# The lo part of every second block of v moves from VectorE to GpSimd, behind a gather

## The reference

```python
expert = jnp.take_along_axis(cand_i, best_pos, axis=-1)
gates = jax.nn.softmax(best_v, axis=-1).astype(h.dtype)
...
ub = jnp.take(u, eb, axis=0)
hid = jax.nn.gelu(jnp.einsum('tkd,td->tk', ub, xb), approximate=False) * gb
vb = jnp.take(v, eb, axis=0)
return jnp.einsum('tk,tkd->td', hid, vb)
```

## Time and profile before

| | us |
|---|---|
| three runs: median (lowest to highest) | 3398.58 (3393.21 to 3403.74) |
| the profiled execution, its own time | 3402.77 |
| its span, first to last instruction | 3401.0 |
| mean granted TensorE clock, share of full speed | 0.973 |
| busy in the span: TensorE matmuls | 3249.2 (96%) |
| VectorE | 2045.5 (60%) |
| ScalarE | 1330.5 (39%) |
| GpSimd | 593.9 (17%) |

### The profile page before, as it was taken

How to read it: one execution, slowest core, us unless ns; L and a number is a source line. 1 busy time by engine, 2 the same in 40 slices (tenths; PEclk the granted TensorE clock), 3 DMA queues, 4 the chain that set the end, 5 groups by cost and what they waited for, 6 DMA issues and landing times.

```text
span 3401.0 us, 40709 instructions
## 1 busy us (share of the span) xinstructions
PE 3249.2 (96%) x16107; PEld 2690.4 (79%) x16107; DVE 2045.5 (60%) x3541; ACT 1330.5 (39%) x2339; POOL 593.9 (17%) x573
## 2 busy tenths in 40 slices
PE   8999999999999999999799998899998999989998
PEld 5764899998888888888688885788787667778887
DVE  5766887876888888888655436445543345443333
ACT  3131238883444444444322225454443124233322
POOL 0001349971222222221000000000000000000000
PEclk9999999999999999999899998999998999989999
DMA  7426244569999999997255422121221122222322
GB/s 258 131 79 230 75 139 160 208 236 343 336 326 334 337 327 331 337 332 278 90 184 185 160 79 89 59 90 63 75 85 58 39 86 76 93 81 94 99 93 80
DMA packets 190206, 574.40 MB, mean 169 GB/s; under 512 B 16576, under 2 KB 82112, under 8 KB 171712
## 3 DMA queue, kind: packets, MB, share of 16 engines
q1 hardware_dynamic: 152144, 367.96, 31.6%
q0 software_dynamic: 37872, 203.84, 16.6%
HBM read 523.89 MB, written 47.84 MB: 168 GB/s over the span
## 4 chain that ended last, share of the span: by engine, by line
PE 82%; DVE 7%; ACT 4%; DMA 3%; POOL 2%; issue 1%; SPq 0%; DVEq 0%; ACTq 0%; POOLq 0%
PE ps L237 11%; PE ps L238 11%; PE ps L239 11%; PE ps L1627 5%; PE ps L1628 5%; PE ps L1626 5%; PE ps L1382 4%; PE ps L1384 4%; PE ps L1383 4%; PE ps L602 2%; PE ps L246 2%; DMA hidden_dram<-peerg_HS 2%; PE ps L171 1%; DMA adaw_AW<-w_ada 1%; PE ps L605 1%; PE ps L2289 1%
## 5 line engine op out<-in xcount | busy, mean ns | idle before, releaser
L229 DVE TENSOR_TENSOR Wl<-W,Wh 128x1024 fp32r<-128x1024 f32 (+2 forms) x337 | 407.6, 1210 | 694.5 <-ACT Wh L217 694.4
L217 ACT ACTIVATE Wh<-W 128x1024 fp32r<-128x1024 f32 x363 | 377.5, 1040 | 553.5 <-PE ps L239 519.2
L1382 PE MATMUL ps<-peer_Hh,Wh 128*128 128x384 f32 x1024 | 348.3, 340 | 2.7 <-DVE Wl L229 1.9
L1384 PE MATMUL ps<-peer_Hh,Wl 128*128 128x384 f32 x1024 | 344.5, 336 | 0.0
L1383 PE MATMUL ps<-peer_Hl,Wh 128*128 128x384 f32 x1024 | 344.0, 336 | 0.0
L1595 POOL DMA_INDIRECT peerv_UV<-peer_uv,peer_EX x128 | 209.3, 1635 | 639.4 <-DVE peer_Y L1663 583.9
L1626 PE MATMUL ps<-peerv_VH,peer_HTh 128*128 128x512 f32 x768 | 299.0, 389 | 2.5 <-DVE peer_HTl L1689 2.5
L1628 PE MATMUL ps<-peerv_VH,peer_HTl 128*128 128x512 f32 x768 | 300.5, 391 | 0.0
L1627 PE MATMUL ps<-peerv_VL,peer_HTh 128*128 128x512 f32 x768 | 300.2, 391 | 0.0
L237 PE MATMUL ps<-f_Hh,Wh 128*128 128x512 f32 x672 | 262.3, 390 | 2.2 <-DVE Wl L229 2.2
L239 PE MATMUL ps<-f_Hh,Wl 128*128 128x512 f32 x672 | 261.5, 389 | 0.0
(11 more groups left out here) (497 smaller groups left out, 6530.2 us busy)
## 6 DMA issues: line engine op xcount, KB each, us to landing
W<-peer_u SPq DMA_DIRECT2D x128, 512.0 KB, 6.9
peerv_VR<-peer_v SPq DMA_DIRECT2D x128, 512.0 KB, 5.3
gates_dram<-peerg_GB SPq DMA_DIRECT2D x12, 2048.0 KB, 7.3
peerv_GR<-gates_dram SPq DMA_DIRECT2D x32, 768.0 KB, 8.3
f_AW<-w_ada POOLq DMA_DIRECT2D x48, 512.0 KB, 4.3
W<-w_gate SPq DMA_DIRECT2D x44, 512.0 KB, 3.2
W<-w_up SPq DMA_DIRECT2D x44, 512.0 KB, 3.3
swa_AW<-w_ada POOLq DMA_DIRECT2D x32, 512.0 KB, 4.3
```

Source lines behind the costliest of these rows:

```text
L217: A.then_inc(e.activation(w_parts(i)[0], w_raw(i), ACT.Copy), ("w_hi", i))
L229: (G if i in lo_on_pool else V).then_inc(e.tensor_tensor(lo, w_raw(i), hi.bitcast(F32), SUB), ("w", i))
L1382: e.matmul(o, hi[:, k, :], H2[0][:, k, 0:TD], start=k == 0, stop=False)
L1384: ins = e.matmul(o, lo[:, k, :], H2[0][:, k, 0:TD], start=False, stop=k == 7)
```

## The change

For odd j, `v_lo(j)` is made by GpSimd. It stands in GpSimd's order right behind the issue of gather j+4 (`v_lo(k - 4)` behind `uv_load(e, k)` for odd k from 5 on), and for j = 125 and 127 behind the last gather. VectorE keeps the even blocks. Who waited for the lo part of v (the load j+3 of v on the sync engine, and `b(j)` on TensorE) waits for GpSimd's semaphore for odd j, through the new helper `v_split`. Each `v_lo(j)` from j = 2 on also waits for `b(j-2)`, whose matmuls read the buffer of `VL` that it writes.

```diff
     def v_load(e, j):
         if j < 128:
             if j >= 3:
-                V.wait_ge(e, ("vl", j - 3))
+                v_split(e, j - 3)
             else:
                 V.wait_ge(e, "EX")
...
+    def v_split(e, j):
+        (G if j % 2 else V).wait_ge(e, ("vl", j))
+
     def v_lo(e, j):
         A.wait_ge(e, ("vh", j))
-        V.then_inc(e.tensor_tensor(VL[:, j % 2, :], VR[:, j % 3, :], VH[:, j % 2, :].bitcast(F32), SUB), ("vl", j))
+        if j >= 2:
+            PE.wait_ge(e, ("b", j - 2))
+        (G if j % 2 else V).then_inc(e.tensor_tensor(VL[:, j % 2, :], VR[:, j % 3, :], VH[:, j % 2, :].bitcast(F32), SUB), ("vl", j))
...
             uv_load(e, k)
+            if k >= 4 and k % 2:
+                v_lo(e, k - 4)
+        for j in (125, 127):
+            v_lo(e, j)
...
                 n = j - 1
                 s = n % 2
-                V.wait_ge(e, ("vl", n))
+                v_split(e, n)
                 V.wait_ge(e, ("htl", n))
...
-            v_lo(e, j)
+            if j % 2 == 0:
+                v_lo(e, j)
             if j:
                 y_add(j - 1)
```

## The result

| | before | after |
|---|---|---|
| median of four runs, us | 3398.19 | 3445.47 |
| lowest to highest | 3393.21 to 3403.74 | 3442.21 to 3448.81 |
| the profiled execution, its own time | 3402.77 | 3442.21 |
| its span | 3401.0 | 3440.4 |
| first matmul of b(0) to first matmul of b(127) | 824.7 | 869.9 |

The changed kernel is slower: 3445.47 against 3398.19, ratio 1.0132 with a 95% interval of 1.012 to 1.0145, so +47 us where 29 were forecast. The stage itself is 45.2 us longer. (The two profiled spans differ by 39.4 only, because behind b(127) this execution of the changed kernel was 6.1 us shorter, 1775.9 against 1781.9, in a part that the change doesn't touch.)

A forecast was written before the change was run, and what follows sets the result against it. TensorE's matmuls were taken to bound the dense stage. New TensorE waits of 22 or 34 us plus 1 at the start gave 23 to 35, middle 29, on a median of 3398.6: 3427.6 us, range 3402 to 3456.

The forecast's parts named there:

- TensorE bounds, no gain possible: In the dense-expert stage TensorE's matmuls set the time without gaps, so moving work off VectorE can gain nothing.
- The relief of 0.7 us: In odd blocks, with the subtraction gone from VectorE, y_add starts sooner and the round is 0.7 us shorter.
- The hold: GpSimd's subtraction shuts out VectorE's instructions that read two SBUF tiles, for 2.11 us each.
- case (a): Subtraction follows the gather with no gap, ahead of htl, and holds VectorE; htl is done 4.77 us after y_add(j-1) ends.
- The round of two blocks: VectorE and ScalarE's ring over two blocks: 11.96 us without gap, plus 1.14 where w_lo is in the even round.
- The round against TensorE: Slower rounds from b(7) to b(19) make TensorE wait 2.4 or 3.7 us in each 14 blocks, 22 or 34 in all.
- The lead before the change: In the kernel before, operands of b(19) were ready at about 67.5 us, 3.0 us early.
- Small items: At the start b(1) waits, +1 us; later loads stay hidden, and the next gather and waits for b(j-2) cost nothing.
- case (b): With a 0.3 us gap behind the gather, GpSimd gets in after htl(j) and holds VectorE from 2.76 to 4.87 us.
- The waits absorb it: Rival: GpSimd's hold falls in VectorE's waits or is partial, so the ring stays ahead; 3399 to 3406 us, chance 0.16.
- GpSimd is shut out too: Rival: GpSimd's subtraction misses the gap behind htl and comes behind tg, 5 us later; 3450 to 3700 us, chance 0.08.
- Faster: Rival: only if TensorE had hidden gaps; 3380 to 3388 us, chance 0.03.

The follow-up runs named there:

- experiment 5: Changed kernel, but GpSimd makes only the 17 blocks with j % 14 = 7 or 13: 3398.48 us, ratio 0.9997 to the kernel before.
- experiment 9: Changed kernel, but in odd blocks GpSimd copies VR into VL instead of subtracting, reading one tile: 3403.28 us, ratio 1.0003 to the kernel before.
- experiment 2: Changed kernel, but in odd blocks GpSimd fills VL by two memsets of zeros and reads nothing: 3404.96 us, ratio 1.0008 to the kernel before.
- experiment 3: Kernel before, plus 62 GpSimd subtractions of one tile from itself into a scratch tile, which no other engine waits for: 3444.33 us, ratio 1.0122.
- 7: Changed kernel, but each of GpSimd's 64 subtractions also waits for tg of its block: 3436.16 us, ratio 1.0108 to the kernel before.
- 8: Changed kernel, but the subtraction stands ahead of the gather's issue in GpSimd's order: 3440.74 us, ratio 1.0118 to the kernel before.
- experiment 4: Changed kernel, but GpSimd makes only the 32 blocks with j % 4 = 1: 3428.3 us, ratio 1.0079 to the kernel before.

## Why the prediction was right, and why it was too low

**TensorE bounds, no gain possible: right.** With the earlier trace rows as they were, no kernel came out faster; the lowest ratios are 0.9997 and 1.0003 (experiments 5 and 9).

**The relief of 0.7 us: right.** It shows in experiment 2 (+0.7 of lead) and in experiment 9, where it pays for a hold of 0.66.

**The hold: right.** Read from one pair of rows of another stage as 2.11 us; it measured 2.03 on an htl. (The prediction set the 2.11 beside an estimate of 2.1 us for the length of a subtraction; 2.11 is the length of the hold, and the subtraction itself takes 2.36 alone and 2.40 here.) The hold was measured alone (experiment 3), without reading (2), with one input (9) and at other steps (7, 8). The Trainium skill, "SBUF — State Buffer", section "Who interferes with whom", says that a VectorE instruction with two SBUF inputs contends with a GpSimd instruction only where that one reads SBUF; the trace agrees at both ends, 0.56 us beside a memset and 1.22 beside a copy.

**Where it falls: right, case (a),** in 51 of 64 blocks: gap 0.02 us, GpSimd's subtraction 2.40 against 2.36, htl ready at 4.80 against 4.77. In two more, 53 and 109, GpSimd came behind the start of htl and held it too. Nine others held tg. The last two, for which the prediction had noted "no gather ahead" and nothing else, held y_add:

```profile
1658.50 3.11 DVE L1672 SCALAR_TENSOR_TENSOR peer_Y<-peerv_UV,peerv_HG,peer_Y 128x1024 f32<-128x1024 f32 x1 [0.81 <-ACT peerv_HG L1655]
```

**The round of two blocks: right,** 13.13 against 13.10.

**The round against TensorE: right in kind, too low in size.** I walked the slower rounds in one line from b(7) to b(19) and had TensorE wait 2.4 us in 14 blocks (operands at 72.9, TensorE at 70.5). Experiment 7, where no tg and no y_add is held, has 3.37. The same stretch one period on, from the end of b(21) to b(33), says where the 0.97 are; there the end of b(21) is at 946.22 (VectorE, then TensorE):

```profile
1017.03 2.60 DVE L1701 TENSOR_TENSOR peer_HTl<-peer_TG,peer_HTh 128x384 fp32r<-128x384 f32 x1 [0.59 <-ACT peer_HTh L1668]
```

```profile
1019.77 0.47 PE L1637 MATMUL ps<-peerv_VH,peer_HTh 128*128 128x512 f32 x1 [0.46 <-DVE peer_HTl L1701]
```

The htl of block 33 is done after 73.4 us and not 72.9: the five rounds take 12.95, 12.93, 13.13, 13.42 and 13.13 us where the forecast had 12.91 twice and 13.10 three times, and the long one is the round in which v_hi(30) waits for b(28), a wait that the walk left out. TensorE would have come after 70.3 us and not 70.5 (kernel before: 936.53 to 1006.84). The handover of 0.14 us was not in the sum, nor the 0.1 us that TensorE loses behind its stops. These add up to 0.94 of the 0.97. That TensorE stands at several blocks and not at one adds nothing to the sum by itself; it makes b(28) later, and with it, probably, the fourth round (no run tells this from the rest).

**The lead before the change: wrong, and not a term of the sum.** The prediction had the operands of b(19) "about 67.5, 3.0 us early". In the trace of before, one period on, the htl is ready at 70.0 and b(33) starts at 70.3. The rounds from v_hi(23) to v_hi(33) take 12.4 us each, and the fourth 13.9, where I had 12.1 and 12.3: v_hi(j) waits for b(j-2), ScalarE stands there for 1.59 us ahead of v_hi(30), and the ring can't run further ahead. I had read these waits (33.5 us in 53 places) as a lead of 0.26 a block; what is left in front of b is 0.27 us in four blocks of 14. The forecast's 2.4 is the slow ring less TensorE's own time and doesn't use the 3.0, so this error did not move it; it is what made the expectation of experiment 4 wrong. Rows that showed it were at hand: the end of htl and the start of b of a few blocks.

**The GELU: not in the prediction.** The tg waits for ScalarE in a block where VectorE, relieved of v_lo, comes sooner than TensorE and ScalarE deliver (experiment 2: 0.71 us sooner). A quarter of a microsecond there lets GpSimd in before tg (tg starts 0.6 and not 0.9 us ahead of the subtraction). 1.3 us in 14 blocks.

**Small items.** b(1) was late by 1.29 us (forecast +1). The loads stayed hidden. GpSimd's next gather didn't wait for its subtraction.

The stage's 45.2 us by these terms: 23 were forecast in case (a) (22 and 1 for the start); the longer wait in each 14 blocks adds 9.7 (experiment 7's stage is 857.4, +32.7); the held tg add 12.5. The forecast's middle of 29 had case (b) in it, which did not occur. The two errors have the same sign, and the range of 3402 to 3456 held 3445 because it also spanned the rivals, not because its bounds knew of them.

**The rivals.** *The waits absorb it* fell: htl is longer in all the odd blocks where it isn't tg or y_add. But its idea, that a hold can fall in a lead, is true for the blocks of experiment 5, and its lateness of VL shows by itself in experiment 2. *GpSimd is shut out too* fell: 64 subtractions have a mean of 2.403 us against 2.36 alone. *Faster* fell.

## What to carry to other kernels

Before moving a step between VectorE and GpSimd, ask of each instruction that runs beside it whether both read SBUF; here GpSimd's subtraction of 2.4 us held a VectorE instruction that came during it until shortly before its end, whether or not anyone waited for the result. Price the lateness block by block, from the end of the last operand to the start of the matmul that reads it, less the handover (0.14 us here); an average of waits, or a walk of one engine's rounds that leaves out who holds it back, gives leads that don't exist (3.0 us where there were 0.29). And where two engines race, look for the blocks in which a result that comes a quarter of a microsecond late turns their order round: that carried a quarter of the cost here.

## What the runs showed of the hardware that I had not expected

- The hold begins ahead of the record of GpSimd's instruction when that stands behind a gather: VectorE instructions recorded up to 0.62 us before the subtraction's start were held for its whole length, those 0.90 before it never. In blocks 53 and 109 even a htl that was recorded 0.24 and 0.53 us ahead of it was held. Why, no record says; what an instruction that starts 0.62 to 0.90 us ahead would meet, no run shows.
- A GpSimd copy with one SBUF input holds a two-input VectorE instruction too: htl 1.22 us beside a copy of 1.06, and 0.56 beside a memset of 0.97. VectorE went on about 0.13 us before the copy's end as recorded (1011.75 less 0.56 is 1011.19; the copy ends at 1011.32), and 0.14 before the subtraction's (1007.40 against 1007.54).
- A GpSimd subtraction of 1024 elements a partition takes 2.40 us from two tiles (64 in the changed kernel) and 1.90 us when both inputs are the same tile (62 in experiment 3; its output is float32 and not fp32r, so the two differ in that too); a copy takes 1.06 (experiment 9).
- GpSimd's subtraction needed no gap to speak of behind the issue of a gather (0.02 us), and its length beside a VectorE that wants SBUF was 2.36 to 2.49 in all kernels, mostly 2.40, against 2.36 alone: the one that holds is hardly slowed.
